# RMSNorm at the layer boundary and at the end: one root per token column, spread by a matmul; last tiles split

## Chip, cores, metric

One NeuronCore of a Trainium2 chip. The metric is the device time of one execution in microseconds; the runs of the kernel before gave 1078.87 us as median of three (1077.52 to 1078.99).

## What is computed

A backbone of two layers over 512 latent and 256 context tokens of width 1024. Layer 0 is a Fourier mixer, layer 1 a bidirectional retention with four heads. Each branch is normed, modulated, gated and projected back; what comes out is the normed latent stream.

```python
def rmsnorm(x, g):
    return x * lax.rsqrt(jnp.mean(x * x, axis=-1, keepdims=True) + EPS) * g
for i in range(2):
    hl = rmsnorm(x, norm_g[i]) * (1.0 + sc_l) + sh_l      # 512 latent tokens
    hc = rmsnorm(ctx, norm_g[i]) * (1.0 + sc_c) + sh_c    # 256 context tokens
    if i == 0:
        ol, oc = fourier_mixer(hl, ...), fourier_mixer(hc, ...)   # both end in @ w_out (2048 x 1024)
    else:
        ol, oc = retention_mixer(hl, hc, ...)
    x = x + gt_l * ol
    if i == 0:
        ctx = ctx + gt_c * oc
return rmsnorm(x, final_g)
```

## The kernel before

Activations lie with features on the 128 partitions and tokens along the free axis: eight feature tiles (KT = 8) of 512 latent columns (LAT) and 256 context columns, together 768 (TOK). Each product is made in three single-precision matmuls of a high and a low part of both operands (`mm3`, L1373 to L1375). The weights come as a stream of slots of 128x1024; each is loaded by the sync engine, converted to its high part by ScalarE (`hi`, L578) and its low part made by VectorE (`lo`, L903), in halves of 512 columns, into a ring of two slots. TensorE waits for the halves (`split`) and frees them (`slot_done`). Every engine executes its own list in order; the order was written by hand, and semaphores join the lists.

Layer boundary. `out_tile` makes one 128-feature tile of the out0 projection: for each of 16 k tiles, three matmuls of the 512 latent columns, then three of the 256 context columns with the same weights, into two accumulator banks. For each finished tile m VectorE adds the gated result to x (`x1_tile`, L1121), ScalarE squares it (L719) and makes a scaled copy tmp_t (L720), and VectorE adds the squares to acc_t (`x1_squares`, L1129). After the last tile TensorE multiplies acc_t by a matrix of ones (L1604 latent, L1606 context). Every partition then holds the sums of all tokens, 128x512 and 128x256. ScalarE roots them to rstd_t (`root`, L743), VectorE inverts them (reciprocal L1153 for the latents, L1175 for the context, before `h1_norm(3)`).

Then h = tmp_t * rstd + shift is made tile by tile: the multiplication for latents on VectorE (`h1_norm`, L1160), for latent tiles 2 and 5 and for all eight context tiles on GpSimd (L520, L525), the high part on ScalarE (`h1_hi`, L751), the low part on VectorE (`h1_low`, L1166). First all eight latent steps, then all eight context steps. Behind them, on ScalarE and on VectorE, stands `used(0)` of head 0, which converts head slot 2. TensorE's `head(0, first=True)` multiplies slots 0 and 1 with the latents (`lat_pair(0, 0, 1)`, one k as soon as `hlo_done` says so), then slots 2 and 3 (`lat_pair(2, 7, 6)`), and then slots 4 and 5 with latents and context.

End. The out1 projection has eight tiles of 512 columns. After each: `x2_tile` (L1335), square on ScalarE (L865), `x2_squares` (L1342). After the last: sums by the matrix of ones (L1700), root (L884), reciprocal (L1362), and the products with the rstd and final_g: five tiles on VectorE (L1365), three on GpSimd (L566). The sync engine stores each tile of 128x512.

Near the start, GpSimd makes an identity of 128x128 (L460, L462) inside the `gate` buffer, after VectorE has finished part of the layer-0 input. VectorE scales it to diagonals (L1053), and TensorE multiplies these by the ones (L1519), which spreads a value per token over all partitions.

## Time and profile before

| | |
|---|---|
| median of 3 runs | 1078.87 us |
| span of the profiled execution | 1077.0 us |
| TensorE matmul | 1007.6 us busy (94%) |
| VectorE | 519.9 us (48%) |
| ScalarE | 408.2 us (38%) |
| GpSimd | 197.6 us (18%) |
| mean granted TensorE clock | 0.976 of full |
| DMA | 98.14 MB, 91 GB/s on average |

The page's second part cuts the span into 40 slices of 27 us and gives the busy share of each engine in tenths; a dip of TensorE's row is where something other than matmuls may set the time. A timeline row gives the start, the length and, in brackets, the idle time of that engine before the row with the instruction that ended it. Rows of one kind that follow each other are merged (x2, x11), so their length is that of all. Matmuls overlap, so the distance between two starts is the cost of one, not its length.

### The profile page before, as it was taken

To read this page: it belongs to the slowest core of one execution; us is meant where nothing else is said; L and a number is where in the kernel's file an instruction comes from. 1 tells how busy PE (TensorE), PEld (TensorE's weight loads), DVE (VectorE), ACT (ScalarE), POOL (GpSimd) and SP (SyncE) were. 2 spreads that over 40 slices of the span, in tenths; PEclk is the share of its full clock that TensorE was granted. 3 is DMA by queue.
4 is the path that set the end of the run, shared out by engine and by line. 5 is a ranking of instruction groups with operands and counts; after the bars stand their busy time and mean duration, and the time that the engine had idled before them with its cause. 6 is when DMAs were issued, how large, how long until landed. Compare 5 with 4: busy or idle time off the path is not lost.

```text
span 1077.0 us, 14382 instructions
## 1 busy us (share of the span) xinstructions
PE 1007.6 (94%) x5186; PEld 840.2 (78%) x5186; DVE 519.9 (48%) x812; ACT 408.2 (38%) x750; POOL 197.6 (18%) x240
## 2 busy tenths in 40 slices
PE   2798999999999999999599999999999999998993
PEld 2678999777777788888488888888888878886882
DVE  5658444533555363332845426542644264446434
ACT  7347433433544343222433323332333233352321
POOL 3006323122443230000400013001300130010001
PEclk9898999999999999999899999999999999998997
DMA  7642112153534352122021102210221021101222
GB/s 275 250 162 74 60 62 97 42 173 119 165 129 148 125 201 93 60 78 78 20 91 66 61 19 79 76 59 19 78 78 58 19 78 58 58 20 59 98 79 78
DMA packets 27417, 98.14 MB, mean 91 GB/s; under 512 B 3664, under 2 KB 3696, under 8 KB 26992
## 3 DMA queue, kind: packets, MB, share of 16 engines
q1 hardware_dynamic: 25632, 90.77, 25.0%
q0 software_dynamic: 1744, 6.84, 1.7%
q8 instruction: 24, 0.39, 0.1%
q14 instruction: 17, 0.14, 0.0%
HBM read 95.48 MB, written 2.10 MB: 91 GB/s over the span
## 4 chain that ended last, share of the span: by engine, by line
PE 83%; DVE 9%; POOL 3%; ACT 2%; DMA 1%; issue 1%; SPq 0%; DVEq 0%; POOLq 0%; ACTq 0%
PE banks L1373 27%; PE banks L1374 27%; PE banks L1375 26%; DVE ring L903 2%; PE banks L1447 2%; ACT ring L578 1%; DVE hreg L1166 1%; POOL gate L541 1%; POOL gate L462 1%; DMA raw<-stream 1%; DVE xreg L1225 1%; DMA gate<-x_rows 1%; DVE gate L1160 1%; DVE hreg L978 1%; DVE xreg L1365 0%
## 5 line engine op out<-in xcount | busy, mean ns | idle before, releaser
L903 DVE TENSOR_TENSOR ring<-raw,ring 128x512 fp32r<-128x512 f32 x320 | 220.2, 718 | 366.7 <-ACT ring L578 365.0
L578 ACT ACTIVATE ring<-raw 128x512 fp32r<-128x512 f32 x320 | 190.0, 626 | 399.4 <-PE banks L1375 382.6
L1373 PE MATMUL banks<-hreg,ring 128*128 128x512 f32 (+1 forms) x800 | 291.2, 364 | 19.8 <-DVE hreg L1166 9.1
L1374 PE MATMUL banks<-hreg,ring 128*128 128x512 f32 (+1 forms) x800 | 287.6, 360 | 0.0
L1375 PE MATMUL banks<-hreg,ring 128*128 128x512 f32 (+1 forms) x800 | 285.7, 357 | 0.0
L1373 PEld LDWEIGHTS banks<-hreg,ring 128*128 128x128 f32 x800 | 151.9, 190 | 56.1 <-DVE ring L903 18.1
L1375 PEld LDWEIGHTS banks<-hreg,ring 128*128 128x128 f32 x800 | 151.5, 189 | 23.3
L1374 PEld LDWEIGHTS banks<-hreg,ring 128*128 128x128 f32 x800 | 151.9, 190 | 22.4 <-issue 1.0
L1373 PE MATMUL banks<-wreg,ring 128*128 128x258 f32 (+2 forms) x288 | 93.1, 323 | 10.3 <-DVE ring L903 9.2
L1374 PE MATMUL banks<-wreg,ring 128*128 128x258 f32 (+2 forms) x288 | 92.7, 322 | 0.0
L1375 PE MATMUL banks<-wreg,ring 128*128 128x258 f32 (+2 forms) x288 | 92.2, 320 | 0.0
L501 POOL TENSOR_TENSOR gate<-xreg,gate 128x257 f32<-128x257 f32 (+1 forms) x64 | 50.2, 814 | 135.3 <-ACT gate L688 126.0
L1373 PE MATMUL banks<-ring,hreg 128*128 128x512 f32 x192 | 74.7, 389 | 0.0
L1374 PE MATMUL banks<-ring,hreg 128*128 128x512 f32 x192 | 74.7, 389 | 0.0
L1375 PE MATMUL banks<-ring,hreg 128*128 128x512 f32 x192 | 74.7, 389 | 0.0
L1373 PEld LDWEIGHTS banks<-wreg,ring 128*128 128x128 f32 x288 | 55.1, 191 | 15.3 <-issue 11.1
L534 POOL TENSOR_TENSOR gate<-gate 128x512 f32<-128x512 f32 x12 | 16.7, 1395 | 250.7 <-ACT gate L768 249.9
L1375 PEld LDWEIGHTS banks<-wreg,ring 128*128 128x128 f32 x288 | 55.0, 191 | 4.2
L1374 PEld LDWEIGHTS banks<-wreg,ring 128*128 128x128 f32 x288 | 55.2, 192 | 3.8
L1373 PE MATMUL banks<-wreg 128*128 128x512 f32 x144 | 56.0, 389 | 0.0
L1374 PE MATMUL banks<-wreg 128*128 128x512 f32 x144 | 56.0, 389 | 0.0
L1375 PE MATMUL banks<-wreg 128*128 128x512 f32 x144 | 56.0, 389 | 0.0
(174 smaller groups left out, 1290.3 us busy)
## 6 DMA issues: line engine op xcount, KB each, us to landing
raw<-stream SPq DMA_DIRECT2D x160, 512.0 KB, 3.3
gate<-x_rows SPq DMA_DIRECT2D x6, 512.0 KB, 9.3
gate<-x_lat POOLq DMA_DIRECT2D x1, 2048.0 KB, 14.4
xreg<-x_lat POOLq DMA_DIRECT2D x1, 2048.0 KB, 7.8
xreg<-tables_in SPq DMA_DIRECT2D x1, 1284.0 KB, 10.2
out<-xreg SPq DMA_DIRECT2D x5, 256.0 KB, 2.6
gate<-x_ctx POOLq DMA_DIRECT2D x1, 1024.0 KB, 18.1
xreg<-x_ctx POOLq DMA_DIRECT2D x1, 1024.0 KB, 11.0
```

The lines of the kernel that those rows point to most:

```text
L462: pool.affine_select(out=ident, in_=ident, compare_op=ALU.not_equal, fill=1.0, base=0, pattern=[[-1, P]], channel_multiplier=1).then_inc(i ...
L501: pool.tensor_tensor(g, y, g, ALU.mult).then_inc(gated, 1)
L534: pool.tensor_tensor(head_rstd, head_rstd, p_f[:, i % 2, :], ALU.add).then_inc(oacc, 1)
L541: pool.tensor_tensor(g, g, p_f[:, i % 2, :], ALU.mult).then_inc(ogated, 1)
L578: act.activation(ring[:, n % 2, 0, c], raw[:, buf, c], ACT.Copy).then_inc(hi_done, 1)
L903: dve.tensor_tensor(ring[:, n % 2, 1, c], raw[:, buf, c], f32(ring[:, n % 2, 0, c]), ALU.subtract).then_inc(split_done, 1)
L978: dve.scalar_tensor_tensor(out=xs[1][:, t, :], in0=x_tok[:, t, :], scalar=tok_rstd[:, t:t + 1], in1=f32(xs[0][:, t, :]), op0=ALU.mult, op1 ...
L1160: dve.tensor_tensor(tmp_t[:, k, 0:LAT], tmp_t[:, k, 0:LAT], rstd_t[:, 0:LAT], ALU.mult).then_inc(t_vec, 1)
L1373: pe.matmul(out, left[0], right[0], start=start, stop=False)
L1374: pe.matmul(out, left[0], right[1], start=False, stop=False)
L1375: return pe.matmul(out, left[1], right[0], start=False, stop=stop)
L1447: last = pe.matmul(bank(7, parts=4), cond[:, k, :], ring[:, par, part, 512 * half:512 * half + 512], start=k == 0 and part == 0, stop=k == ...
```

## The change

The sums of squares are taken per token as a column: a matmul whose stationary operand is a 128-token block of acc_t and whose moving operand is one column of ones gives 128 tokens on 128 partitions (`token_sums`). ScalarE roots a 128 x n block with one column per 128 tokens (n is 4 for the latents, 2 for the context or a half of the latents) and VectorE inverts it; VectorE multiplies an identity by each column (`token_rstd`, result `spread`, 128 x 128n), and TensorE multiplies the matrix of ones by these diagonals (`token_rows`). For the latents this is written to two banks: one is read by VectorE directly, the other is copied to rstd_t by ScalarE (`rstd_copy`) for GpSimd.

The last out0 tile does all 16 k of the latent columns first and then all 16 k of the context columns (`out_last`); the latent sums are taken inside the context part, after k = 9. The context sums are taken inside the first pair of head 0, after k = 4; their root stands on ScalarE after `h1_hi(4)`, their inversion on VectorE before `h1_norm(7)`, `token_rows(1)` on TensorE after the whole first pair, and the copy for GpSimd on ScalarE after the last latent `h1_hi`. The conversion of head slots 0 and 1 moves behind the last out0 tile's context part on both engines.

The last out1 tile is made in two halves of 256 tokens, each with its own sums, root, spread and output products. Stores are one transfer for several tiles of a half: tiles 3 to 5 and 6 to 7 from the sync engine, tiles 0 to 2 from ScalarE's queue. The identity gets a buffer of its own and is made without the wait for the layer-0 input.

The diff, cut (declarations, the `parts` argument of `x1_tile` and `x1_squares` and unchanged lines are left out):

```diff
+        ident = sb("ident", [P, P])
...
+        spread = gate[:, 6144:6144 + TOK].rearrange("p (t n) -> p t n", t=TT)
+        tok_rms = small[:, 0:TT]
...
-            for m in range(KT):
-
-                if m < POOL_TILES:
-                    sp.wait_ge(out_pool, m + 1)
-                    src = tmp_t[:, m, 0:LAT]
-                else:
-                    sp.wait_ge(out_vec, m - POOL_TILES + 1)
-                    src = x3[:, m, :]
-                sp.dma_start(out[m], src).then_inc(s_out, 16)
-            sp.wait_ge(s_out, 16 * KT)
+            for h in range(2):
+                c = slice(LAT // 2 * h, LAT // 2 * (h + 1))
+                for a, b in ((POOL_TILES, 6), (6, KT)):
+                    sp.wait_ge(out_vec, (KT - POOL_TILES) * h + b - POOL_TILES)
+                    sp.dma_start(out[a:b].rearrange("m p t -> p m t")[:, :, c],
+                                 x3[:, a:b, c]).then_inc(s_out, 16)
+            sp.wait_ge(s_out, 16 * 6)
...
-            pool.wait_ge(hf_lo, KT + 1)
-            pool.memset(ident, 0.0).then_inc(ident_set, 1)
+            pool.memset(ident[:, :], 0.0).then_inc(ident_set, 1)
...
-            pool.affine_select(out=ident, in_=ident, compare_op=ALU.not_equal, fill=1.0, base=0,
+            pool.affine_select(out=ident[:, :], in_=ident[:, :], compare_op=ALU.not_equal, fill=1.0, base=0,
...
             gate_head(HEADS - 1, (0, 2))
-            pool.wait_ge(rstd_done, 3)
-            for m in range(POOL_TILES):
-                pool.wait_ge(gained, m + 1)
-                pool.tensor_tensor(tmp_t[:, m, 0:LAT], tmp_t[:, m, 0:LAT], rstd_t[:, 0:LAT],
-                                   ALU.mult).then_inc(out_pool, 1)
+            for h in range(2):
+                c = slice(LAT // 2 * h, LAT // 2 * (h + 1))
+                pool.wait_ge(rstd_done, 3 + h)
+                for m in range(POOL_TILES):
+                    pool.wait_ge(gained, m + 1)
+                    pool.tensor_tensor(tmp_t[:, m, c], tmp_t[:, m, c], rstd_t[:, c],
+                                       ALU.mult).then_inc(out_pool, 1)
         @block.scalar
...
             hi("out0", 5, SLOT_OUT0 + 5)
-            def x1_tile(m, q):
-
-                for v, (a, b, x) in enumerate(((0, LAT, x3), (LAT, TOK, xc3))):
+            def root(n, first, tiles):
+                act.wait_ge(sum_sq_done, n + 1)
+                act.activation(tok_rms[:, first:first + tiles], bank(4, tiles, first), ACT.Sqrt,
+                               scale=1.0 / D, bias=eps[:, :]).then_inc(root_done, 1)
+
+            def rstd_copy(n, a, b, src):
+                act.wait_ge(rows_spread, n + 2)
+                act.activation(rstd_t[:, a:b], src, ACT.Copy).then_inc(rstd_done, 1)
+
+            def x1_tile(m, q, parts=(0, 1)):
+
+                for v in parts:
+                    a, b, x = ((0, LAT, x3), (LAT, TOK, xc3))[v]
                     act.wait_ge(x1_done, 2 * m + (v + 1 + 4))
...
             act.activation(dk[:, 1, 0:1], eps[:, :], ACT.Sqrt).then_inc(warm, 1)
+            x1_tile(7, 1, (0,))
+            root(0, 0, 4)
+            x1_tile(7, 1, (1,))
             hi("head", 0, SLOT_HEAD)
             hi("head", 1, SLOT_HEAD + 1)
-            x1_tile(7, 1)
-
-            def root(n, a, b):
-                act.wait_ge(sum_sq_done, n + 1)
-                act.activation(rstd_t[:, a:b], banks[:, a:b], ACT.Sqrt, scale=1.0 / D,
-                               bias=eps[:, :]).then_inc(root_done, 1)
             def h1_hi(k, v, a, b):
...
                                bias=mod1[:, 8 + k, v:v + 1]).then_inc(hhi_done, 1)
-            root(0, 0, LAT)
-            root(1, LAT, TOK)
+            rstd_copy(0, 0, LAT, bank(7))
             for k in range(KT):
                 h1_hi(k, 0, 0, LAT)
+                if k == 4:
+                    root(1, 4, 2)
+            rstd_copy(1, LAT, TOK, bank(3, CTX))
             for k in range(KT):
...
-            x2_sq(7, 1)
-            act.wait_ge(sum_sq_done, 3)
-            act.activation(rstd_t[:, 0:LAT], bank(0), ACT.Sqrt, scale=1.0 / D,
-                           bias=eps[:, :]).then_inc(root_done, 1)
+            act.wait_ge(acc_done, 7 + (2 * KT + 4))
+            for h in range(2):
+                c = slice(LAT // 2 * h, LAT // 2 * (h + 1))
+                act.wait_ge(x2_half, h + 1)
+                act.activation(sq_t[:, 1, c], x3[:, KT - 1, c], ACT.Square).then_inc(sq_half, 1)
+                act.wait_ge(sum_sq_done, 3 + h)
+                act.activation(tok_rms[:, 2 * h:2 * h + 2], bank(0, 2, 2 * h), ACT.Sqrt, scale=1.0 / D,
+                               bias=eps[:, :]).then_inc(root_done, 1)
+                act.wait_ge(rows_spread, 5 + 2 * h)
+                act.activation(rstd_t[:, c], bank(3 + 2 * h, LAT // 2), ACT.Copy).then_inc(rstd_done, 1)
+            for h in range(2):
+                c = slice(LAT // 2 * h, LAT // 2 * (h + 1))
+                act.wait_ge(out_pool, POOL_TILES * (h + 1))
+                act.dma_start(out[0:POOL_TILES].rearrange("m p t -> p m t")[:, :, c],
+                              tmp_t[:, 0:POOL_TILES, c]).then_inc(s_out, 16)
...
+            dve.wait_ge(hf_lo, 12)
...
-                dve.tensor_scalar(diag[:, t, :], ident, tok_rstd[:, t:t + 1], None,
+                dve.tensor_scalar(diag[:, t, :], ident[:, :], tok_rstd[:, t:t + 1], None,
...
-            for q in range(2):
-                if q == 0:
-                    lo("out0", 14, SLOT_OUT0 + 14)
-                    lo("out0", 15, SLOT_OUT0 + 15)
-                else:
-                    lo("head", 0, SLOT_HEAD)
-                x1_tile(6 + q, (bank(3 + 2 * q), bank(4 + 2 * q, CTX)), SLOT_OUT0 + 13 + 2 * q)
-                x1_squares(6 + q, q)
+            lo("out0", 14, SLOT_OUT0 + 14)
+            lo("out0", 15, SLOT_OUT0 + 15)
+            x1_tile(6, (bank(3), bank(4, CTX)), SLOT_OUT0 + 13)
+            x1_squares(6, 0)
+
+            def token_rstd(n, first, tiles):
+
+                dve.wait_ge(root_done, n + 1)
+                r = tok_rms[:, first:first + tiles]
+                link(dve.reciprocal(r, r))
+                dve.tensor_tensor(spread[:, first:first + tiles, :],
+                                  ident[:, :].unsqueeze(1).to_broadcast([P, tiles, P]),
+                                  r.unsqueeze(2).to_broadcast([P, tiles, P]),
+                                  ALU.mult).then_inc(spread_done, 1)
+
+            last_banks = bank(5), bank(6, CTX)
+            dve.wait_ge(last_lat, 1)
+            x1_tile(7, last_banks, None, (0,))
+            x1_squares(7, 1, (0,))
+            dve.wait_ge(glo, FT)
+            dve.wait_ge(ident_set, 2)
+            token_rstd(0, 0, 4)
+            x1_tile(7, last_banks, SLOT_OUT0 + 15, (1,))
+            x1_squares(7, 1, (1,))
+            lo("head", 0, SLOT_HEAD)
...
-            dve.wait_ge(root_done, 1)
-            dve.reciprocal(rstd_t[:, 0:LAT], rstd_t[:, 0:LAT]).then_inc(rstd_done, 1)
-            dve.wait_ge(rstd_done, 1)
+            dve.wait_ge(rows_spread, 1)
...
-                    dve.tensor_tensor(tmp_t[:, k, 0:LAT], tmp_t[:, k, 0:LAT], rstd_t[:, 0:LAT],
+                    dve.tensor_tensor(tmp_t[:, k, 0:LAT], tmp_t[:, k, 0:LAT], bank(2),
...
             for k in range(KT):
-                if k == 1:
-                    dve.wait_ge(root_done, 2)
-                    dve.reciprocal(rstd_t[:, LAT:TOK], rstd_t[:, LAT:TOK]).then_inc(rstd_done, 1)
+                if k == 5:
+                    token_rstd(1, 4, 2)
                 h1_norm(k + 2)
...
-            for q in range(2):
-                if q == 0:
-                    lo("out1", 14, SLOT_OUT1 + 14)
-                    lo("out1", 15, SLOT_OUT1 + 15)
-                x2_tile(6 + q, 7 - q, SLOT_OUT1 + 13 + 2 * q)
-                x2_squares(6 + q, q)
-            dve.wait_ge(root_done, 3)
-            dve.reciprocal(rstd_t[:, 0:LAT], rstd_t[:, 0:LAT]).then_inc(rstd_done, 1)
-            dve.wait_ge(rstd_done, 3)
-            for m in range(POOL_TILES, KT):
-                dve.scalar_tensor_tensor(out=x3[:, m, :], in0=x3[:, m, :], scalar=g_final[:, m:m + 1],
-                                         in1=rstd_t[:, 0:LAT], op0=ALU.mult,
-                                         op1=ALU.mult).then_inc(out_vec, 1)
+            lo("out1", 14, SLOT_OUT1 + 14)
+            lo("out1", 15, SLOT_OUT1 + 15)
+            x2_tile(6, 7, SLOT_OUT1 + 13)
+            x2_squares(6, 0)
+
+            def last_out(h):
+
+                c = slice(LAT // 2 * h, LAT // 2 * (h + 1))
+                dve.wait_ge(rows_spread, 4 + 2 * h)
+                for m in range(POOL_TILES, KT):
+                    dve.scalar_tensor_tensor(out=x3[:, m, c], in0=x3[:, m, c],
+                                             scalar=g_final[:, m:m + 1], in1=bank(1 + h, LAT // 2),
+                                             op0=ALU.mult, op1=ALU.mult).then_inc(out_vec, 1)
+
+            for h in range(2):
+                c = slice(LAT // 2 * h, LAT // 2 * (h + 1))
+                if h == 0:
+                    dve.wait_ge(last_half, 1)
+                else:
+                    dve.wait_ge(slot_done, 2 * SLOTS + DONE0)
+                dve.scalar_tensor_tensor(out=x3[:, KT - 1, c], in0=bank((6, 4)[h], LAT // 2),
+                                         scalar=mod1[:, 24 + KT - 1, 0:1], in1=x3[:, KT - 1, c],
+                                         op0=ALU.mult, op1=ALU.add).then_inc(x2_half, 1)
+                dve.wait_ge(sq_half, h + 1)
+                dve.wait_ge(acc_done, KT - 1 + (2 * KT + 5))
+                dve.tensor_tensor(acc_t[:, c], acc_t[:, c], sq_t[:, 1, c], ALU.add).then_inc(acc_half, 1)
+                if h == 0:
+                    dve.wait_ge(glo, 2 * FT)
+                token_rstd(2 + h, 2 * h, 2)
+                last_out(h)
...
-            with pe.Fori(2, 4) as jj:
+            with pe.Fori(2, 3) as jj:
...
-            pe.wait_ge(acc_done, 2 * KT + 3)
-            pe.matmul(bank(0), ones[:, :], acc_t[:, 0:LAT], start=True, stop=True).then_inc(sum_sq_done, 1)
-            pe.wait_ge(acc_done, 2 * KT + 4)
-            pe.matmul(bank(1, CTX), ones[:, :], acc_t[:, LAT:TOK], start=True,
-                      stop=True).then_inc(sum_sq_done, 1)
-
-
+            pe.wait_ge(x1_done, 14)
+            out_tile(SLOT_OUT0 + 12, both_chunks(bank(3), bank(4, CTX)), g0)
+            pe.wait_ge(x1_done, 16)
+
+            def out_last(t, chunks, g, arrived, between):
+
+                for n, (a, b, o) in enumerate(chunks):
+                    for kk in range(FT):
+                        if n == 0 and kk % 4 == 0:
+                            split(t + kk // 8, kk // 4 % 2)
+                        last = mm3(o, part_of(kk // 8, P * (kk % 8)), (g(kk, 0)[:, a:b], g(kk, 1)[:, a:b]),
+                                   kk == 0, kk == FT - 1)
+                        if n == 1 and kk % 4 == 3:
+                            last.then_inc(slot_done, 1)
+                        if n == 1:
+                            between(kk)
+                    if n == 0:
+                        last.then_inc(arrived, 1)
+
+            def token_sums(first, tiles, out):
+
+                for t in range(first, first + tiles):
+                    last = pe.matmul(out[:, t:t + 1], acc_t[:, P * t:P * t + P], ones[:, 0:1],
+                                     start=True, stop=True)
+                last.then_inc(sum_sq_done, 1)
+
+            def token_rows(n, first, tiles, outs):
+
+                pe.wait_ge(spread_done, n + 1)
+                for out in outs:
+                    for t in range(tiles):
+                        last = pe.matmul(out[:, P * t:P * t + P], ones[:, :], spread[:, first + t, :],
+                                         start=True, stop=True)
+                    last.then_inc(rows_spread, 1)
+
+            def lat_sums(kk):
+                if kk == 9:
+                    pe.wait_ge(acc_done, 2 * KT + 3)
+                    pe.wait_ge(x1_done, 18)
+                    token_sums(0, 4, bank(4))
+
+            out_last(SLOT_OUT0 + 14, both_chunks(bank(5), bank(6, CTX)), g0, last_lat, lat_sums)
+            token_rows(0, 0, 4, (bank(2), bank(7)))
...
+            def ctx_sums():
+                pe.wait_ge(acc_done, 2 * KT + 4)
+                token_sums(4, 2, bank(4))
+
...
                 if first:
-                    pe.wait_ge(root_done, 2)
-                    lat_pair(0, 0, 1, KT)
+                    lat_pair(0, 0, 1, KT, between=ctx_sums)
+                    token_rows(1, 4, 2, (bank(3),))
+                    pe.wait_ge(rstd_done, 1)
                 else:
...
-            with pe.Fori(2, 4) as jj:
+            with pe.Fori(2, 3) as jj:
...
-            pe.wait_ge(acc_done, 3 * KT + 5)
-            pe.matmul(bank(0), ones[:, :], acc_t[:, 0:LAT], start=True, stop=True).then_inc(sum_sq_done, 1)
+            pe.wait_ge(x1_done, 2 * 3 + (2 * KT + 3))
+            out_tile(SLOT_OUT1 + 12, ((0, LAT, bank(7)),), g1)
+            pe.wait_ge(x1_done, 2 * 3 + (1 + 2 * KT + 3))
+
+            def half_sums(kk):
+                if kk == 8:
+                    pe.wait_ge(acc_half, 1)
+                    token_sums(0, 2, bank(0))
+                if kk == 14:
+                    token_rows(2, 0, 2, (bank(1), bank(3)))
+
+            out_last(SLOT_OUT1 + 14, ((0, LAT // 2, bank(6, LAT // 2)),
+                                      (LAT // 2, LAT, bank(4, LAT // 2))), g1, last_half, half_sums)
+            pe.wait_ge(acc_half, 2)
+            token_sums(2, 2, bank(0))
+            token_rows(3, 2, 2, (bank(2), bank(5)))
```

## Rows read from the trace of the kernel before

**Rows 1.** The page, part 4: the chain that ended last, its shares by engine
```profile
PE 83%; DVE 9%; POOL 3%; ACT 2%; DMA 1%; issue 1%; SPq 0%; DVEq 0%; POOLq 0%; ACTq 0%
```

**Rows 2.** Timeline, VectorE, layer boundary: start us, us, engine, line, operation, idle before, releaser
```profile
514.07 1.14 DVE L1121 SCALAR_TENSOR_TENSOR xreg<-banks,mod,xreg 128x512 f32<-128x512 f32 x2 [7.04 <-PE banks L1375]
...
518.15 3.35 DVE L1153 RECIPROCAL gate<-gate 128x512 f32<-128x512 f32 x1
521.53 2.36 DVE L1160 TENSOR_TENSOR gate<-gate 128x512 f32<-128x512 f32 x2
...
535.69 5.72 DVE L1166 SCALAR_TENSOR_TENSOR hreg<-gate,mod,hreg 128x512 fp32r<-128x512 f32 x11
541.33 2.48 DVE L903 TENSOR_TENSOR ring<-raw,ring 128x512 fp32r<-128x512 f32 x4
```

**Rows 3.** Timeline, TensorE, layer boundary
```profile
525.72 0.76 PE L1373 MATMUL banks<-hreg,ring 128*128 128x512 f32 x1 [7.90 <-DVE hreg L1166]
...
530.41 0.63 PE L1373 MATMUL banks<-hreg,ring 128*128 128x512 f32 x1
530.84 0.63 PE L1374 MATMUL banks<-hreg,ring 128*128 128x512 f32 x1
...
532.74 0.39 PE L1375 MATMUL banks<-hreg,ring 128*128 128x512 f32 x1
532.97 0.40 PE L1373 MATMUL banks<-hreg,ring 128*128 128x512 f32 x1
...
542.07 0.50 PE L1373 MATMUL banks<-hreg,ring 128*128 128x512 f32 x1 [0.72 <-DVE ring L903]
```

**Rows 4.** Timeline, GpSimd, layer boundary: the eight context norms
```profile
527.31 9.05 POOL L525 TENSOR_TENSOR gate<-gate 128x256 f32<-128x256 f32 x8 [2.29 <-DVE gate L1175]
```

**Rows 5.** Windows: stretch, length, busy us of each engine, PEclk, DMA share, GB/s
```profile
521.00:522.00 1.00, 0.00 (x0) 0.00 (x0) 0.96 (x2) 0.00 (x0) 0.41 (x1) 0.59 0.01 4
```

**Rows 6.** Timeline, all engines, the end of the kernel
```profile
1059.23 0.75 DVE L1335 SCALAR_TENSOR_TENSOR xreg<-banks,mod,xreg 128x512 f32<-128x512 f32 x1 [7.48 <-PE banks L1375]
...
1066.70 6.51 DVE L1365 SCALAR_TENSOR_TENSOR xreg<-xreg,small,gate 128x512 f32<-128x512 f32 x5
```

**Rows 7.** Timeline, VectorE, early in the kernel
```profile
97.07 1.28 DVE L1053 TENSOR_SCALAR gate<-gate,dist 128x128 f32<-128x128 f32 x6 [0.19 <-POOL gate L462]
```

**Rows 8.** Timeline, TensorE, early: 258-column matmuls and the ones x diagonal passes
```profile
99.14 0.28 PE L1374 MATMUL banks<-wreg,ring 128*128 128x258 f32 x1
99.26 0.28 PE L1375 MATMUL banks<-wreg,ring 128*128 128x258 f32 x1
99.76 0.36 PE L1373 MATMUL banks<-wreg,ring 128*128 128x258 f32 x1 [0.22 <-DVE wreg L909]
...
102.71 1.50 PE L1519 MATMUL banks<-gate,ones 128*128 128x128 f32 x12
103.97 0.42 PE L1373 MATMUL banks<-hreg,wreg 128*128 128x386 f32 x1
```

**Rows 9.** Groups by form: line, engine, operation, shapes, count, busy us, mean ns, idle
```profile
L1121 DVE SCALAR_TENSOR_TENSOR xreg<-banks,mod,xreg 128x256 f32 x4 | 1.9, 474 | 0.0
...
L961 DVE RECIPROCAL dist<-dist 128x1 f32<-128x1 f32 x6 | 0.9, 158 | 3.4 <-ACT dist L601 3.4
...
L578 ACT ACTIVATE ring<-raw 128x512 fp32r<-128x512 f32 x320 | 190.0, 626 | 399.4 <-PE banks L1375 382.6 <-DMA raw<-stream 11.5 <-PE banks L1447 4.4
...
L751 ACT ACTIVATE hreg<-gate,mod 128x256 fp32r<-128x256 f32 x8 | 3.3, 494 | 0.0
...
L601 ACT ACTIVATE dist<-dist,eps 128x1 f32<-128x1 f32 x6 | 1.8, 294 | 0.2
...
L551 POOL TENSOR_TENSOR xreg<-xreg 128x512 f32<-128x512 f32 x8 | 10.4, 1297 | 0.0
```

**Rows 10.** Timeline, 650 to 665 us: VectorE reads a bank while GpSimd works
```profile
653.53 1.27 DVE L1190 TENSOR_TENSOR gate<-banks,gate 128x512 f32<-128x512 f32 x2
...
653.69 1.29 POOL L549 TENSOR_TENSOR xreg<-xreg 128x512 f32<-128x512 f32 x1 [10.08 <-DVE xreg L1225]
```

17 lines of the change are left out of this document (11 added, 6 removed).

## Prediction

> **What bounds the kernel now.** The chain of work that ended last belongs to TensorE for 83% of the span [rows 1], and TensorE is busy nearly everywhere at the full clock. A change of norms can therefore only act where TensorE stands still. I read the page's slices for the two dips (the layer boundary at 514 to 542 us and the end from 1059 us), then the timelines of each engine there, then the groups by form for durations.
>
> At the boundary VectorE starts on the last out0 tile at 514.07, the moment TensorE has finished it. It converts its last head-slot part at 518.1, takes 3.35 us for a reciprocal over 128x512, and begins the norms at 521.53 [rows 2]. TensorE starts layer 1 at 525.72, and its second pair of columns of head 0 at 542.07, after 0.72 us of waiting for a ring part (L903) [rows 3]. That part is queued on VectorE behind all sixteen h1_low steps (the last eleven start at 535.69 and the ring follows at 541.33) [rows 2]. So until 542.07 the bound is VectorE's queue, not TensorE. Beside it GpSimd does the eight context norms from 527.31 to 536.36, while the latent half is still going on [rows 4]. That overlap is what matters below.
>
> TensorE's granted clock falls to half within 521 to 522, after about 3.4 us in which it had done nothing (its sums ended 7.90 us before 525.72, at 517.8) [rows 3, 5]. After the restart matmuls stand 0.43 us apart (530.41, 530.84), later 0.23 (532.74, 532.97) [rows 3]. Between 525.72 and 531.3 some 12 matmuls ran at 1.2 GHz instead of 2.4, 0.2 us each: a restart from a cold clock costs 2.4 us.
>
> At the end, the last matmul is over at 1059.2. From there a chain of whole 512-token steps: x2 at 1059.23, square, add, sums, root, a reciprocal as long as the first, and then five output tiles on VectorE from 1066.70 for 6.51 us (1.3 us each while GpSimd works beside it) and then 3.8 us until the span's end at 1077.0 [rows 6].
>
> **Start of the kernel.** The identity moves to a buffer of its own and is made some 50 us earlier. VectorE no longer waits for it at 97.07, 0.19 us [rows 7]; TensorE waited 0.22 us at 99.76 for the weights that VectorE makes next [rows 8]. I take -0.2 (bounds 0 and -0.3). GpSimd stood idle where the instruction goes now.
>
> **Boundary, up to the first matmul of layer 1.** The latent chunk of the last tile goes first, the context chunk after it, so the same matmuls end where they did. Between them TensorE makes four column sums: 4 x 2 passes of at most one short pass. Twelve passes of 128 columns took 1.26 us from 102.71 to 103.97, 0.105 each [rows 8], so 0.9 us (from 0.3, as one column streams in less, to 2.8, if none overlaps the next: one alone takes 1.50 less eleven starts of 0.105, 0.35). x1 of the latents, squares, sums, the small root, the small reciprocal (158 ns for one column [rows 9]) and the spread over the identity are hidden under the 5.6 us of the context chunk. TensorE ends the tile at about 515.0.
>
> What is late next is not the norm but VectorE's queue: x1 of the context waits for the chunk's end (0.47), ScalarE squares and scales it (two steps of under 0.49), and only then converts four ring halves, 0.6 each, which VectorE follows (0.69 for the last) [rows 9]. 515.0 + 0.5 + 0.9 + 2.4 + 0.7 = 519.4 against 521.53: of the 3.35 us reciprocal only 2.1 us come back.
>
> The first two norms read a bank now. VectorE's steps with one operand in a bank stayed at 0.63 us apiece while GpSimd worked beside them (653.53, two in 1.27; GpSimd's 1.29 unchanged) [rows 10], whereas the same norms from SBUF took 1.18 each [rows 2]. So the first h1_low ends about 2.8 us after the norms begin, instead of 4.0, and TensorE starts at 522.2 (was 525.72). It has been idle 5.4 us, longer than the 3.4 us above, and starts at half clock, as before.
>
> **Boundary, step 5.** At the half clock TensorE does k = 0, 1 until 527.4, then k = 2 to 4 at 1.38 each until 531.5, then the context sums (0.45). VectorE is ahead of it now, as it has no long reciprocal and cheaper norms. But its next step, token_rstd(1), sits in front of norm 7 and h1_low 5, and waits for the root of those context sums. Behind TensorE's sums at 532.0 come the root (0.29, as for one column), reciprocal (0.16) and spread (0.45), norm 7 (0.62), h1_low 5 (0.7) and hops [rows 9, 10]: TensorE idles 2.4 us and does k = 5 to 7 from 534.4 to 538.5.
>
> **Boundary, the context half: the term that decides.** Before, the context's rstd was ready at 527.3 [rows 4] and GpSimd multiplied under the latent half. Now token_rows(1) stands on TensorE behind the whole first pair of head 0. Only after it come ScalarE's copy to rstd_t, which stands behind all latent h1_hi, GpSimd's eight norms, h1_hi and h1_low of the context; and behind these, on ScalarE and on VectorE, the conversion of head slot 2, without which TensorE can't start the second pair. Nothing covers this chain:
> - token_rows(1), 4 passes of 0.11: 539.0. ScalarE's copy with hops 0.5: 539.5.
> - GpSimd, eight 128x256 products. They took 1.13 each beside a busy VectorE [rows 4]. Alone, 128x512 takes 1.30 [rows 9], so half of it at least 0.65; with some fixed part I take 0.74. VectorE would have one 0.47 us step per tile here, so I take 0.74 + 7 x 1.0 = 7.7: 547.3 (bounds 545.4 and 548.6).
> - h1_hi 0.5, h1_low 0.5, the ring half 0.7, hops: 1.8. TensorE restarts at 549.1, against 542.07: +7.0 us.
> - This idle time is 10 us, so the clock is at half once more: +2.4 us, which before did not occur here.
>
> Together the boundary gives +9.4 us. Later TensorE is unbroken in head 0, so it is all carried on.
>
> For the contention, the row (1.13 beside a VectorE that never paused) bounds the step from above. The Trainium skill, page "SBUF — State Buffer", section "Who interferes with whom", says more: a VectorE instruction with two SBUF inputs and a GpSimd instruction that reads SBUF exclude one another wholly. By that each step would take 0.74 + 0.43, the context chain would be 1.2 us longer, and the total 1086.6. The same section has a VectorE instruction with one SBUF input free of GpSimd, and the 653.53 row agrees.
>
> **End.** The last tile is done in halves of 256 tokens. Same columns in all; 258 columns stood 0.12 apart (99.14, 99.26) [rows 8], so 96 matmuls need 11.4 instead of 10.9 us. The sums of half 0 (0.45) and its rows (0.9, before the last k) come on top: TensorE ends at about 1061.1 (was 1059.2). Half 0: rows at about 1060.3, then VectorE's five products, 0.47 each with a bank operand [rows 9]: 1062.6. The chain of half 1 stands behind these on VectorE, 1.5 us later than its matmuls allow. Then x2 0.47, square 0.45, add 0.45, sums 0.7, root 0.3, reciprocal and spread 0.65, rows 0.7 (slow clock), hops 0.3: 1066.6. VectorE's products end at 1069.0; the second copy for GpSimd is behind the rows' second set, 1067.9, and its three products of 0.74 end at 1070.1. With the 3.8 us that followed the last product before, and 0.4 for larger transfers of 1 KB pieces (no row shows one: bounds -0.3 and +1.5), the span ends 2.7 us earlier (bounds 1.2 and 3.7).
>
> **The sum.** +9.4 - 2.7 - 0.2 = +6.5 us on the execution of 1077.0: 1083.5. The median of the runs is 1.9 us above that profile, so 1085.4 us. Unknown terms: GpSimd's rate -1.9/+1.3; the second cold restart -2.4; the wait at k = 5, if the clock falls in it too, +2.4; the end -1/+1.5. This gives 1082 to 1089.
>
> **Rivals.**
> - The context chain is hidden (the forecast's main step is wrong): if slot 2 were ready when the first pair ends, the pair would follow at 539.0, 3.1 us earlier than before, and the time would be 1078.9 - 3.1 - 0.2 - 2.7 = 1072.9. For it: the code gives the chain the same covers as before by name. Against: the in-order queues. It decides once the chain from 538.5 takes under 3.5 us, where GpSimd alone needs 5.2. Chance 0.08.
> - The chain is there but cheap: products at 0.7, warm restart, the full gain at the end: 1085.4 - 1.9 - 2.4 - 1 = 1080.1, no difference to be told. Chance 0.12.
> - The clock falls a third time, at k = 5: 1087.8. Speaking for it, at 521 to 522 it fell after 3.4 us idle; against, this wait is 2.4. Part of the forecast's range, 0.15.
> - The change doesn't do what it says: the reciprocals don't shorten, as the small steps' fixed costs add up. Each is 0.16 to 0.45, far below 3.35; inside the range too.
>
> **How the numbers follow.** Forecast (slower, 1082 to 1089) 0.80, within it the centre; the no-difference case 0.12; the faster one 0.08. A measurement here tells about 0.2%, 2.2 us. For 8 in 10 the range reaches from 1080.0 to 1089.5.
>
> **What would show it.** Right: TensorE's first hreg matmul near 522, an idle time of 2 to 3 us before k = 5, a wait of 8 to 11 us before the second pair with GpSimd's eight products inside it, a granted clock at half after it, a last product near 1070. Wrong: context products that start before TensorE has ended the first pair, or a second pair that starts by 543.

## The result and the profile after

The changed kernel took 1088.05 us (median of four runs, 1084.60 to 1088.15) beside 1078.93 us for the kernel before on the same chip: a ratio of 1.0078, 95% interval 1.0058 to 1.0097. Measured again on another chip it took 1084.81 us (six runs, 1083.66 to 1088.11) beside 1079.53: 1.0047, 1.0029 to 1.0065. It is slower, by 5 to 9 us. The profiled execution took 1084.60 us, with a span of 1082.8 us, and TensorE's mean granted clock was 0.973 (0.976 before).

The chain that ended last, page part 4, shares by engine. Beside [rows 1], "issue" went from 1% to 3% and VectorE from 9% to 7%:

```profile
PE 84%; DVE 7%; POOL 3%; issue 3%; ACT 2%; DMA 1%; SPq 0%; POOLq 0%; DVEq 0%; ACTq 0%
```

The timeline of TensorE at the boundary after the change (it answers to [rows 3]; in brackets the idle time and what ended it):

```profile
510.68 0.95 PE L1683 MATMUL banks<-ones,gate 128*128 128x1 f32 x8
...
521.37 0.76 PE L1431 MATMUL banks<-hreg,ring 128*128 128x512 f32 x1 [5.70 <-DVE hreg L1208]
...
530.79 0.50 PE L1683 MATMUL banks<-ones,gate 128*128 128x1 f32 x4
533.55 0.80 PE L1431 MATMUL banks<-hreg,ring 128*128 128x512 f32 x1 [2.27 <-DVE hreg L1208]
534.15 0.63 PE L1432 MATMUL banks<-hreg,ring 128*128 128x512 f32 x1
534.58 0.63 PE L1433 MATMUL banks<-hreg,ring 128*128 128x512 f32 x1
...
539.32 0.61 PE L1692 MATMUL banks<-gate,ones 128*128 128x128 f32 x4
549.15 0.77 PE L1431 MATMUL banks<-hreg,ring 128*128 128x512 f32 x1 [9.22 <-DVE ring L926]
```

There are three waits here: 5.70 us before the layer's first matmul (7.90 before [rows 3]), 2.27 us at k = 5 behind the context's column sums (L1683), and 9.22 us before the second pair. The last one was 0.72 us before [rows 3].

The other engines in the same stretch, each from its own timeline (VectorE answers to [rows 2], GpSimd to [rows 4]):

```profile
512.06 0.18 DVE L1179 RECIPROCAL small<-small 128x4 f32<-128x4 f32 x1 [2.63 <-ACT small L718]
...
518.22 1.28 DVE L1202 TENSOR_TENSOR gate<-gate,banks 128x512 f32<-128x512 f32 x2
...
531.62 0.17 DVE L1179 RECIPROCAL small<-small 128x2 f32<-128x2 f32 x1 [5.95 <-ACT small L718]
...
546.83 0.57 DVE L1208 SCALAR_TENSOR_TENSOR hreg<-gate,mod,hreg 128x256 fp32r<-128x256 f32 x1 [0.29 <-ACT hreg L761]
547.69 0.48 DVE L1208 SCALAR_TENSOR_TENSOR hreg<-gate,mod,hreg 128x256 fp32r<-128x256 f32 x1 [0.29 <-ACT hreg L761]
548.31 2.50 DVE L926 TENSOR_TENSOR ring<-raw,ring 128x512 fp32r<-128x512 f32 x4
```

```profile
540.42 6.69 POOL L526 TENSOR_TENSOR gate<-gate 128x256 f32<-128x256 f32 x8 [19.75 <-ACT gate L723]
```

```profile
539.96 0.38 ACT L723 ACTIVATE gate<-banks 128x256 f32<-128x256 f32 x1 [6.37 <-PE banks L1692]
541.18 0.51 ACT L761 ACTIVATE hreg<-gate,mod 128x256 fp32r<-128x256 f32 x1 [0.83 <-POOL gate L526]
541.87 0.51 ACT L761 ACTIVATE hreg<-gate,mod 128x256 fp32r<-128x256 f32 x1 [0.17 <-POOL gate L526]
542.82 0.51 ACT L761 ACTIVATE hreg<-gate,mod 128x256 fp32r<-128x256 f32 x1 [0.45 <-POOL gate L526]
543.69 0.51 ACT L761 ACTIVATE hreg<-gate,mod 128x256 fp32r<-128x256 f32 x1 [0.36 <-POOL gate L526]
```

The 3.35 us reciprocal is gone (0.18), and VectorE's norms start at 518.22 instead of 521.53 (the whole boundary lies 0.94 us earlier in this execution, see the table below). But the context's chain now begins only when TensorE has ended the pair: rows 539.32, copy 539.96, GpSimd 540.42 to 547.11, ring part 548.31, TensorE 549.15. GpSimd had been idle for 19.75 us; before, it did the same eight products at 527.31 [rows 4].

The granted clock by stretch (columns as in [rows 5]: length, busy us of the five engines, then PEclk):

```profile
531.50:533.50 2.00, 0.00 (x0) 0.00 (x0) 1.85 (x5) 1.93 (x4) 0.00 (x0) 1.00 0.00 0
534.00:536.00 2.00, 2.00 (x6) 1.52 (x6) 0.82 (x2) 0.00 (x0) 0.00 (x0) 0.50 0.03 8
...
538.00:542.00 4.00, 1.93 (x11) 1.49 (x9) 0.28 (x1) 1.03 (x3) 1.57 (x3) 1.00 0.00 0
...
544.00:549.00 5.00, 0.00 (x0) 0.00 (x0) 3.47 (x7) 3.57 (x8) 3.12 (x4) 0.50 0.00 0
549.00:552.00 3.00, 2.85 (x7) 2.33 (x8) 3.00 (x7) 0.74 (x2) 0.00 (x0) 0.50 0.41 115
```

Each new wait is followed by a stretch at half clock (1.2 GHz). In the short one the granted clock still stands at 1.00 until 533.50, as the wait ends; the matmuls behind it run at 0.50.

The end, from the timelines of VectorE, TensorE and GpSimd (they answer to [rows 6]), and from the page's part 6 the two stores that ScalarE issues (size and median time from issue to landing):

```profile
1058.70 0.75 DVE L1376 SCALAR_TENSOR_TENSOR xreg<-banks,mod,xreg 128x512 f32<-128x512 f32 x1
...
1069.47 2.05 DVE L1406 SCALAR_TENSOR_TENSOR xreg<-xreg,small,banks 128x256 f32<-128x256 f32 x5 [1.71 <-PE banks L1692]
1071.43 0.48 DVE L1416 SCALAR_TENSOR_TENSOR xreg<-banks,mod,xreg 128x256 f32<-128x256 f32 x1
...
1076.15 2.05 DVE L1406 SCALAR_TENSOR_TENSOR xreg<-xreg,small,banks 128x256 f32<-128x256 f32 x5 [1.31 <-PE banks L1692]
```

```profile
1068.82 1.05 PE L1692 MATMUL banks<-gate,ones 128*128 128x128 f32 x8
1072.87 1.01 PE L1683 MATMUL banks<-ones,gate 128*128 128x1 f32 x4 [2.64 <-DVE gate L1421]
1074.89 2.07 PE L1692 MATMUL banks<-gate,ones 128*128 128x128 f32 x8 [1.01 <-DVE gate L1180]
```

```profile
1077.46 2.09 POOL L569 TENSOR_TENSOR gate<-gate 128x256 f32<-128x256 f32 x3 [5.00 <-ACT gate L903]
```

```profile
out<-gate ACTq DMA_DIRECT2D x2, 384.0 KB, 2.7
```

**Where the time went.** Two moments cut the span the same way in every kernel here: TensorE's first 258-column matmul after the modulation, and the start of VectorE's x2 of out1 tile 6 (L1335 before, L1376 after). The three stretches, and the time from the latent column sums (L1683 x8) to that x2 for the kernels that have them, read from each kernel's timelines:

| kernel | to the first 258-column matmul | from there to x2 of tile 6 | rest of the span | latent sums to x2 of tile 6 |
|---|---|---|---|---|
| before | 96.50 | 953.13 | 27.37 | |
| changed | 95.56 | 963.14 | 24.10 | 548.02 |
| changed, again | 97.01 | 962.81 | 24.08 | 547.29 |
| only the boundary | 95.61 | 963.02 | 27.37 | 547.73 |
| only the end | 99.13 | 952.97 | 23.90 | |
| context sums early | 96.40 | 959.83 | 23.87 | 544.98 |
| wait filled | 95.33 | 960.33 | 24.04 | 545.15 |
| ring first | 96.72 | 958.83 | 23.75 | 543.32 |
| whole context chain early | 96.58 | 946.26 | 24.06 | 531.18 |
| same, filled | 97.00 | 946.40 | 22.80 | 530.79 |
| same, end woven | 94.62 | 946.19 | 23.19 | 531.09 |
| reordered | 94.34 | 948.67 | 23.19 | 531.61 |
| reordered, filled | 94.55 | 945.68 | 23.17 | 530.33 |

So between the two profiled executions the change is -0.94, +10.01 and -3.27 us, together the 5.8 us of the spans. The first column varies from 94.34 to 99.13 among the twelve rows below "before", whose code is the same in that stretch, so it measures no part of the change. It goes with the granted clock of one early stretch: from 50 to 60 us that was 1.00 in the six executions with 94.34 to 95.61 us in this column, the changed kernel's first among them, 0.83 to 0.86 in the six with 96.40 to 97.01, and 0.70 in "only the end".

### The profile page after: what moved, and what is told of

Its sections match the earlier page's. It is cut to its first block, busy times and chain, and to the rows that moved or that the text cites. A ratio compares the mean times of both kernels' runs of the same rounds, so it can differ in the third digit from the quotient of the medians.

```text
span 1082.8 us, 14568 instructions
## 1 busy us (share of the span) xinstructions
PE 1016.4 (94%) x5284; PEld 853.1 (79%) x5284; DVE 508.4 (47%) x824; ACT 410.0 (38%) x756; POOL 186.8 (17%) x243
## 4 chain that ended last, share of the span: by engine, by line
PE 84%; DVE 7%; POOL 3%; issue 3%; ACT 2%; DMA 1%; SPq 0%; POOLq 0%; DVEq 0%; ACTq 0%
PE banks L1431 28%; PE banks L1432 27%; PE banks L1433 27%; DVE ring L926 3%; PE banks L1505 2%; ACT ring L581 1%; DMA raw<-stream 1%; POOL gate L542 1%; DVE hreg L1051 1%; DVE xreg L1266 1%; POOL gate L526 1%; DVE hreg L1001 1%; DVE gate L1231 0%; POOL gate L535 0%; POOL xreg L552 0%
## 5 line engine op out<-in xcount | busy, mean ns | idle before, releaser
L1431 PE MATMUL banks<-hreg,ring 128*128 128x512 f32 (+1 forms) x812 | 295.0, 363 | 27.2 <-DVE ring L926 16.8
L1432 PE MATMUL banks<-hreg,ring 128*128 128x512 f32 (+1 forms) x812 | 291.1, 359 | 0.0
L1433 PE MATMUL banks<-hreg,ring 128*128 128x512 f32 (+1 forms) x812 | 289.1, 356 | 0.0
L1431 PEld LDWEIGHTS banks<-hreg,ring 128*128 128x128 f32 x812 | 155.2, 191 | 61.4 <-issue 19.2
L1433 PEld LDWEIGHTS banks<-hreg,ring 128*128 128x128 f32 x812 | 154.8, 191 | 23.1
L1432 PEld LDWEIGHTS banks<-hreg,ring 128*128 128x128 f32 x812 | 155.3, 191 | 22.5 <-issue 1.0
L1431 PE MATMUL banks<-wreg,ring 128*128 128x258 f32 (+2 forms) x292 | 94.3, 323 | 9.2 <-DVE ring L926 9.0
L1432 PE MATMUL banks<-wreg,ring 128*128 128x258 f32 (+2 forms) x292 | 93.8, 321 | 0.0
L1433 PE MATMUL banks<-wreg,ring 128*128 128x258 f32 (+2 forms) x292 | 93.3, 319 | 0.0
L1431 PEld LDWEIGHTS banks<-wreg,ring 128*128 128x128 f32 x292 | 56.3, 193 | 14.2 <-issue 10.2
L535 POOL TENSOR_TENSOR gate<-gate 128x512 f32<-128x512 f32 x12 | 16.8, 1396 | 250.7 <-ACT gate L780 250.0
L1433 PEld LDWEIGHTS banks<-wreg,ring 128*128 128x128 f32 x292 | 56.3, 193 | 3.9
L1432 PEld LDWEIGHTS banks<-wreg,ring 128*128 128x128 f32 x292 | 56.4, 193 | 3.7
```

Source lines behind the costliest of these rows:

```text
L535: pool.tensor_tensor(head_rstd, head_rstd, p_f[:, i % 2, :], ALU.add).then_inc(oacc, 1)
L1431: pe.matmul(out, left[0], right[0], start=start, stop=False)
L1432: pe.matmul(out, left[0], right[1], start=False, stop=False)
L1433: return pe.matmul(out, left[1], right[0], start=False, stop=stop)
```

## The experiments

**Only the end**: the kernel before with the identity's own buffer and the last out1 tile in halves.

```diff
+        ident = sb("ident", [P, P])
...
-            dve.wait_ge(root_done, 3)
-            dve.reciprocal(rstd_t[:, 0:LAT], rstd_t[:, 0:LAT]).then_inc(rstd_done, 1)
...
+            for h in range(2):
...
+                token_rstd(2 + h, 2 * h, 2)
+                last_out(h)
```

> The end of the changed kernel and its own identity buffer, with the layer boundary of the kernel before. If the sum of the prediction holds, the end and the start give -2.7 and -0.2 us: 1076.0 us on 1078.9 (the traces of before and after, cut at the add of out1 tile 6, say -3.3: 1075.4). Rival: the end gives nothing by itself, as the last transfers and the second half's chain take it back: 1078.7.

1074.67 us (six runs, 1074.19 to 1077.84), ratio 0.9951 (0.9938 to 0.9964). The end alone is a gain: 27.37 to 23.90 us in the table. (The profiled execution was the longest of the six, 1077.84 us, by its first stretch.)

**Only the boundary**: the changed kernel with the end of the kernel before.

```diff
-            for h in range(2):
...
-                token_rstd(2 + h, 2 * h, 2)
-                last_out(h)
...
+            dve.wait_ge(root_done, 3)
+            dve.reciprocal(rstd_t[:, 0:LAT], rstd_t[:, 0:LAT]).then_inc(rstd_done, 1)
```

> The boundary of the changed kernel, with the end of the kernel before. Forecast of the sum: +9.4 - 0.2, so 1088.1 us; the second pair of head 0 starts 7 us later than in before, behind a wait of 9 us with GpSimd's eight context products in it. Rival: most of the loss of the changed kernel lies elsewhere (more instructions outside loops, the end): under 1083.

1087.76 us (six runs, 1086.46 to 1089.21), ratio 1.0071 (1.0057 to 1.0086). The middle stretch is 963.02 against 953.13, the end unchanged to the hundredth. The two halves of the change are thus separate, and the loss is all in the boundary. The two ratios add up to +0.22%, with some 0.2% of uncertainty, which fits the +0.47% of the second measurement and not the +0.78% of the first; the stretches of the profiled executions do add up (963.14 and 24.10 beside 963.02 and 23.90).

**The whole context chain early**: the changed kernel, with the context's column sums, root, reciprocal, spread and rows ahead of the first pair, and ScalarE's copy behind its first h1_hi. Nothing is added, only moved.

```diff
# TensorE
-                    lat_pair(0, 0, 1, KT, between=ctx_sums)
+                    ctx_sums()
                     token_rows(1, 4, 2, (bank(3),))
+                    lat_pair(0, 0, 1, KT)
# VectorE
+            token_rstd(1, 4, 2)
             dve.wait_ge(rows_spread, 1)
...
-                if k == 5:
-                    token_rstd(1, 4, 2)
# ScalarE
+            root(1, 4, 2)
             rstd_copy(0, 0, LAT, bank(7))
...
-                if k == 4:
-                    root(1, 4, 2)
-            rstd_copy(1, LAT, TOK, bank(3, CTX))
+                if k == 0:
+                    rstd_copy(1, LAT, TOK, bank(3, CTX))
```

> The changed kernel, with the context's column sums, root, inversion, spread and rows all made before the first pair of head 0, in the time in which TensorE waits for h1 anyway, and ScalarE's copy of the context rows after h1_hi(0). If the serial context chain behind the first pair is the cause, both waits (2.3 us at k = 5, 9.2 us before the second pair) and one or two cold restarts go: the rival's sum, 1072.9 us, plus 0.6 for VectorE's extra steps before the first norm: 1073.5. If the contention or the banks as operands are the cause, the loss stays: over 1080.

1067.29 us (six runs, 1066.06 to 1071.26), ratio 0.9887 (0.9869 to 0.9905): 12 us below the kernel before, 17 to 21 below the changed one. Its timelines, TensorE, VectorE and GpSimd:

```profile
520.74 0.96 PE L1691 MATMUL banks<-gate,ones 128*128 128x128 f32 x4 [3.75 <-DVE gate L1180]
522.97 0.77 PE L1430 MATMUL banks<-hreg,ring 128*128 128x512 f32 x1 [1.26 <-DVE hreg L1209]
```

```profile
519.39 1.29 DVE L1180 TENSOR_TENSOR gate<-ident,small 128x256 f32<-128x256 f32 x1
```

```profile
522.39 7.68 POOL L526 TENSOR_TENSOR gate<-gate 128x256 f32<-128x256 f32 x8 [0.57 <-ACT gate L723]
```

GpSimd's eight products again run under the latent half, and TensorE does not wait in either place. The first matmul comes 11.31 us after the latent sums instead of 10.69, so the move costs 0.6 us ahead of the layer. The result is 6 us better than I had expected, and the fault was in the expectation: it started from the forecast's 538.5 us for the end of the first pair, a time that contains the wait at k = 5. That wait and its half clock went too. From the rows: 539.32 to 549.15 is 9.83 us, its restart 2.0 (ten matmuls 0.43 instead of 0.23 us apart), 530.79 to 533.55 is 2.76, its restart 1.4 (seven such), less 0.6: 15.4 of the 16.8 us in the table's last column. Where the other 1.4 us went stays open.

**Context sums early, the rest late**: the same with the rows and the copy left behind the first pair, so that only the wait at k = 5 is taken away.

```diff
# against the changed kernel
-                    lat_pair(0, 0, 1, KT, between=ctx_sums)
+                    ctx_sums()
+                    lat_pair(0, 0, 1, KT)
                     token_rows(1, 4, 2, (bank(3),))
```

> The changed kernel, with the context's column sums, root, inversion and spread made before the first pair of head 0, but its rows, ScalarE's copy and all behind them still after the pair. It parts the two waits. The wait at k = 5 (2.27 us) and the half clock after it (534 to 537, 1.5 us) go, less 0.6 us of steps before the first norm: 3 us less than the changed kernel. The wait of 9.2 us and its cold restart stay. If instead the contention of GpSimd with VectorE were the main loss, nothing changes.

1082.05 us (twelve runs, 1079.58 to 1084.61), ratio 1.0024 (1.0011 to 1.0036), 2.8 us below the changed kernel measured beside it. The second wait is untouched:

```profile
545.88 0.77 PE L1429 MATMUL banks<-hreg,ring 128*128 128x512 f32 x1 [9.22 <-DVE ring L925]
```

With the 0.6 us paid ahead of the layer taken off, the wait at k = 5 and its half clock are worth 3 us (963.0 to 959.8 in the table; by the last column 2.3 to 3.0), the late rows and copy the other 13.6 (959.83 to 946.26).

**The wait filled**: nine 512-column matmuls, whose result nothing uses, on TensorE between the rows and the second pair. All else as changed.

```diff
                     token_rows(1, 4, 2, (bank(3),))
+                    for _ in range(9):
+                        pe.matmul(bank(5), ones[:, :], acc_t[:, 0:LAT], start=True, stop=True)
                     pe.wait_ge(rstd_done, 1)
```

> The changed kernel, with nine matmuls of 512 columns on ones and acc_t into a free bank, their result unused, put into TensorE's 9.2 us wait before the second pair. They shorten no chain. If the clock's fall is worth 2.4 us there, the second pair runs at full clock and the time falls by 2.4 us (-0.2%) against the changed kernel; if the cost lies in the wait alone, it doesn't move.

1081.71 us (twelve runs, 1079.26 to 1085.07), ratio 1.0017 (1.0004 to 1.0029). TensorE's timeline and the window of the wait:

```profile
539.53 7.89 PE L1725 MATMUL banks<-gate,ones 128*128 128x512 f32 x18
548.93 0.47 PE L1431 MATMUL banks<-hreg,ring 128*128 128x512 f32 x1 [1.51 <-DVE ring L926]
```

```profile
544.00:549.00 5.00, 3.49 (x9) 1.26 (x8) 3.68 (x7) 3.59 (x8) 2.90 (x4) 1.00 0.00 0
549.00:556.00 7.00, 7.00 (x31) 5.79 (x32) 4.94 (x8) 1.53 (x4) 2.53 (x2) 1.00 0.47 150
```

The second pair comes when it came before (548.93, 549.15), but at the full clock. Latent sums to x2 of tile 6 is 545.15 against 548.02 and 547.29: the second cold restart costs 2.1 to 2.9 us, as the forecast had it (2.4). The chain itself sets the start of the pair.

**The changed kernel again**, on the same chip as "context sums early" and the next two:

> The changed kernel itself once more, on the chip of the three that follow, so that they can be held against it. Its first runs gave 1084.6 and three times 1088.1, the mean clock 0.973 and 0.970: expect 1087 us, and longer runs to be those with the lower mean clock (0.003 of 1083 us is 6.5 us more at half speed, worth 3.2 us). If the length doesn't follow the clock, the spread has another cause.

1084.81 us (1083.66 to 1088.11), 1.0047; I had expected 1087. Both new waits are there again to the hundredth (9.22, 2.27). Its runs lie at 1084 to 1086 with a clock of 0.972 or 0.973, and one at 1088.11 with 0.970, as three of the first four did. So the longer run is the one with the lower clock, as expected. The kernel before does likewise, 1077 to 1081.5. No trace was taken of a longer run of either kernel. The one trace of a long run, "only the end" (1077.84 us on a median of 1074.67), has the excess in the first 100 us, where TensorE's clock fell early on (the table's first column); whether that holds for the other long runs stays open.

**The early chain, filled**: four unused matmuls in the 3.75 us wait and one behind it.

> The version with the early context rows (1067.3 us), with four unused matmuls of 512 columns in TensorE's 3.75 us wait before the context rows, and one behind them. If the half clock after that wait costs time (11 matmuls 0.43 us apart instead of 0.23), the clock stays up and the time falls by up to 2.2 us: 1065.1. Rival: TensorE at full clock then only waits for h1_low, one step each 1.3 to 2 us, and nothing is gained: 1067.3.

1067.25 us (four runs, 1066.67 to 1068.04), ratio 0.9881, against 1067.29 without. The clock stayed at 1.00 through the boundary, yet next to nothing was gained up to the end (530.79 beside 531.18 in the table's last column), because TensorE, now sooner, met VectorE's queue:

```profile
536.78 0.47 PE L1430 MATMUL banks<-hreg,ring 128*128 128x512 f32 x1 [1.61 <-DVE ring L926]
```

It is the bound of the kernel before once more (0.72 us at 542.07, [rows 3]): a ring part behind all sixteen h1_low. The time didn't fall to the 1065.1 that a full clock alone would give; the rival that I had named held.

**The end woven**: the early chain, and in the last tile x2 and add of half 1 put between the output products of half 0; the second rows go first to the bank that ScalarE copies.

```diff
+            last_x2(0)
+            last_add(0)
...
+            last_out(0, POOL_TILES, 5)
+            last_x2(1)
+            last_out(0, 5, 6)
+            last_add(1)
+            last_out(0, 6, KT)
```

> The version with the early context rows, with the end reordered: VectorE's x2, add of the second half go in between the five products of the first half, and the second half's rows go to ScalarE's bank first. If the second half's chain is bound by its place behind the first half's products on VectorE, as the prediction has it, x2 of half 1 comes 1.1 us earlier and the end some 1 to 1.3 us: 1066.2. If its bound is the last matmul or the stores, it stays at 1067.3.

1066.05 us (four runs, 1065.58 to 1066.60), ratio 0.9872 (0.9854 to 0.9891). VectorE's timeline:

```profile
1045.29 0.48 DVE L1415 SCALAR_TENSOR_TENSOR xreg<-banks,mod,xreg 128x256 f32<-128x256 f32 x1 [2.35 <-PE banks L1443]
...
1052.37 0.48 DVE L1415 SCALAR_TENSOR_TENSOR xreg<-banks,mod,xreg 128x256 f32<-128x256 f32 x1
```

x2 of half 1 starts 7.08 us after that of half 0 instead of 8.24 (1063.19 to 1071.43 in the changed kernel), and the rest of the span is 23.19 against 24.06 us: 0.9 of the 1.5 us that the forecast had put on this queue. The difference to the early chain alone lies within the intervals of the medians; the traces show it, the times do not. And the clock matters as much at this place. The filled early chain has the unwoven end and needs only 22.80 us for it, less than the woven one. Its last rows ran at the full clock, 1.20 us where those of the other kernels, the woven ones included, took 2.07 or 2.08:

```profile
1059.19 1.20 PE L1691 MATMUL banks<-gate,ones 128*128 128x128 f32 x8 [1.01 <-DVE gate L1180]
```

That is the one of the eight traces with the unwoven end in which the clock did not fall there. No run says why.

**The ring first**: the changed kernel, with the conversion of head slots 2 and 3 moved ahead of the context's copy, h1_hi and h1_low on ScalarE and VectorE. This asks whether the queue behind which slot 2 stands is the cause, rather than the lateness of the context's rstd.

```diff
# ScalarE
+            hi("head", 2, SLOT_HEAD + 2)
+            hi("head", 3, SLOT_HEAD + 3)
             rstd_copy(1, LAT, TOK, bank(3, CTX))
# VectorE
+            lo("head", 2, SLOT_HEAD + 2)
+            lo("head", 3, SLOT_HEAD + 3)
             for k in range(KT):
                 h1_low(k, 1, LAT, TOK)
```

> The changed kernel, with nothing moved but the conversions of head slots 2 and 3: on ScalarE and on VectorE they now stand before the context's copy, h1_hi and h1_low, not behind them. The context chain is as long as it was and still follows the first pair. If the loss is the place of the ring conversions in the two queues behind that chain, the wait of 9.2 us before the second pair and its cold restart (2.4 us) go, and the chain hides under the second pair's 11 us, a last 0 to 1 us of it perhaps before the third pair: 1084.8 - 9.2 - 2.4 + 0.5 = 1073.7. If TensorE needed the context's parts themselves, or the chain were lengthened by the same amount, the time stays near 1084.

1079.96 us (twelve runs, 1078.92 to 1084.53), ratio 1.0022 (1.0006 to 1.0038): some 4 us won in the trace (543.32 beside 547.29 and 548.02 in the table; 2.7 by the two ratios), not the 11 expected. The wait before the second pair is gone, so the second pair itself needs nothing of the context. But the next one took its place, before the third pair. ScalarE, GpSimd, VectorE and TensorE:

```profile
540.45 0.63 ACT L581 ACTIVATE ring<-raw 128x512 fp32r<-128x512 f32 x1 [2.13 <-PE banks L1441]
540.99 0.37 ACT L723 ACTIVATE gate<-banks 128x256 f32<-128x256 f32 x1
```

```profile
541.43 7.03 POOL L526 TENSOR_TENSOR gate<-gate 128x256 f32<-128x256 f32 x8 [19.21 <-ACT gate L723]
```

```profile
549.44 2.47 DVE L1272 TENSOR_TENSOR xreg<-banks,gate 128x512 f32<-128x512 f32 x4
```

```profile
556.62 0.77 PE L1439 MATMUL banks<-hreg,ring 128*128 128x512 f32 x1 [4.86 <-DVE ring L930]
```

The second half of slot 3 can be converted only when TensorE releases its place at the pair's end (ScalarE 540.45). Behind it stands the context's copy (540.99), which is no later than it was: 28.8 us after the latent sums, 29.3 in the changed kernel. GpSimd, h1_low, the rotation (549.44) and the next ring part follow it in turn, and all of that is longer than the second pair covers. My expectation had looked at the first consumer only. The late rstd is the cause; the order behind it decides which pair of columns pays.

**Reordered, cold and filled**: end_woven's code with the context's root, reciprocal and spread ahead of the conversion of slot 1, and slot 2 converted ahead of the context's h1_low; the second kernel adds the five unused matmuls.

```diff
# VectorE
-            lo("head", 1, SLOT_HEAD + 1)
             token_rstd(1, 4, 2)
+            lo("head", 1, SLOT_HEAD + 1)
...
+            lo("head", 2, SLOT_HEAD + 2)
             for k in range(KT):
                 h1_low(k, 1, LAT, TOK)
```

> The version with early context rows and the reordered end (1066.1 us), with the context's root and spread before the conversion of slot 1, so that the spread runs before GpSimd starts (0.43 us instead of 1.29), and slot 2 converted before the context's h1_low. TensorE starts about 0.7 us earlier and never waits for slot 2; its restart is still cold: 1065.3.

> The same, with five unused matmuls in TensorE's wait before layer 1. With the late start alone (1067.3 without and with them) the full clock only brought a wait of 1.6 us for slot 2. That slot now is early, so the full clock should count here: 2 us less, 1063.5. If h1_low paces TensorE's first pair at either clock, there is no gain: 1065.3.

1067.12 us (0.9891, 0.9873 to 0.9909) and 1065.71 us (0.9884, 0.9865 to 0.9903), where I had expected 1065.3 and 1063.5. The reordering won nothing: TensorE's first matmul comes 11.5 us after the latent sums in both, not 0.7 us sooner than the 11.3 of the early chain. VectorE:

```profile
516.54 1.29 DVE L928 TENSOR_TENSOR ring<-raw,ring 128x512 fp32r<-128x512 f32 x2 [0.49 <-ACT ring L581]
...
517.94 0.42 DVE L1182 TENSOR_TENSOR gate<-ident,small 128x256 f32<-128x256 f32 x1
518.28 2.35 DVE L928 TENSOR_TENSOR ring<-raw,ring 128x512 fp32r<-128x512 f32 x2
```

The spread takes 0.42 us instead of the 1.29 it took beside GpSimd, but the two ring steps behind it now meet GpSimd instead and take 2.35 us, where the two ahead of it took 1.29. The contention was moved, not removed. With the wait filled, the table's last column is the shortest of all (530.33). End woven and this one are some 1.2% faster than the kernel before and are not told apart by their times.

**The identity late**: the kernel before, its identity in a buffer of its own but still made where it was. One run, and one of the kernel before beside it.

```diff
+        ident = sb("ident", [P, P])
...
-            pool.affine_select(out=ident, in_=ident, ...
+            pool.affine_select(out=ident[:, :], in_=ident[:, :], ...
```

> The kernel before, with the identity in a buffer of its own but made at the old place, after VectorE's ninth low part (L1028). GpSimd's affine select took 9.63 us there in before and 0.29 us in the changed kernel, where VectorE was idle at its start. If VectorE's unbroken row of steps with two SBUF operands holds GpSimd off, it takes 9.6 us again; if it was the place of the buffer, 0.3 us.

1079.62 us beside 1078.31, no difference that two single runs can tell. GpSimd's instruction in this kernel, and VectorE's beside it; then the same instruction where the changed kernel has it:

```profile
88.40 9.64 POOL L462 TENSOR_SCALAR_AFFINE_SELECT ident<-ident 128x128 f32<-128x128 f32 x1
```

```profile
84.87 10.61 DVE L1028 SCALAR_TENSOR_TENSOR hreg<-gate,amul,hreg 128x256 fp32r<-128x256 f32 x32
95.39 2.49 DVE L903 TENSOR_TENSOR ring<-raw,ring 128x512 fp32r<-128x512 f32 x4
```

```profile
34.95 0.29 POOL L463 TENSOR_SCALAR_AFFINE_SELECT ident<-ident 128x128 f32<-128x128 f32 x1
```

The long time doesn't come from the buffer. It goes with the moment, or with what the other engines do at it: the instruction ends at 98.04, just after the last of VectorE's unbroken run of 36 steps (97.88), and at 34.95 VectorE was idle.

## Why the prediction was right

It said 1085.4 us, 1080.0 to 1089.5, slower; the two medians are 1088.05 and 1084.81. The profiled span is 1082.8 us, forecast 1083.5. Without the first stretch, which the change doesn't set, the spans differ by +6.7 us, forecast +6.5 with the start's -0.2. The terms behind it hold one by one, but the boundary cost 0.6 more and the end gained 0.6 more than forecast, so that the sum is closer than its terms. Times of before are shifted by the 0.94 us of the first stretch where two kernels are compared.

- **What bounds the kernel** held: only TensorE's waits at the boundary and the end moved the time. In "only the boundary" and "only the end" each stands alone.
- **Start, -0.2.** The identity's instruction shrank from 9.63 to 0.29 us and VectorE's 0.19 us wait went. The 0.94 us by which this stretch was shorter is within what the same code varies by (the clock from 50 to 60 us was 0.83 before and 1.00 after), so the term is not tested.
- **First matmul of layer 1, 522.2 (-3.5).** Measured 521.37, and 525.72 - 0.94 before: -3.4. The forecast's path held in kind: VectorE turned to the norms at 518.22 (forecast 519.4, less the shift 518.5), with the ring parts in its way and not the reciprocal. The norms with a bank operand took 0.64 each beside GpSimd, as [rows 10] said. The page "SBUF — State Buffer" of the Trainium skill, section "Who interferes with whom", has a VectorE instruction with one SBUF input free of GpSimd; these rows agree.
- **Wait at k = 5, 2.4.** It was 2.27, for the reason given (token_rstd(1) behind the context sums). But the clock fell at its end, and seven matmuls ran at the half clock: +1.4 us. The forecast had this as a rival with 0.15 and took the cheaper case, because the wait was shorter than the 3.4 us of [rows 5]. That was the weak step: 2.27 us of waiting behind 0.5 us of one-column sums were enough here, in all five traces that have this wait, some 5 us after TensorE had come back to the full clock. Whether that short stretch mattered was not tried; the 2.23 us wait of the kernel before, at the boundary behind a long stretch of matmuls, left the clock at 1.00. Wait and restart together are 3 us by the run that moved the sums ahead.
- **The context chain, 538.5 to 549.1, is the term that decided**, and the first rival (hidden chain, 1072.9) fell. The chain was where the forecast put it, and shorter: 9.83 us from rows to restart, forecast 10.6. GpSimd took 6.69 us, forecast 7.7: the size of this term was off by 1.0. ScalarE's h1_hi follow GpSimd one by one and show its step: 0.69 us where VectorE's first step hardly overlapped (541.18 to 541.87), 0.95 once (542.82) and 0.87 from then on (543.69). So the step of 0.74 alone was near, the 1.0 beside VectorE too high. VectorE's own step went from 0.48 (547.69, alone) to 0.57. By the exclusion that the same page of the Trainium skill states for a VectorE instruction with two SBUF inputs the step would be 0.69 + 0.48, some 1.2; the rows show 0.87, and the measurement decides: they slow each other by 0.18 and 0.09, and the 1086.6 us worked out from that rule was not the way it went.
- **Second cold restart, +2.4.** Measured 2.0 in the rows and 2.1 to 2.9 by filling the wait.
- The boundary in sum: 549.15 against 542.07 - 0.94 is +8.0 (forecast +7.0: pair ended 1.8 later by the clock fall and small steps, chain 0.8 shorter), and 2.0 for the restart, +10.0 against +9.4.
- **End, -2.7 (1.2 to 3.7).** Measured -3.3. Half 0 went as forecast (x2 of tile 6 to the last product 12.8 us, forecast 13.0). From x2 of half 1 to GpSimd's last product took 8.1, forecast 7.5: the column sums and the first set of rows ran at the half clock and took 1.0 us each (1.01, and half of 2.07 for the two sets), where the forecast had 0.7 each, so VectorE's products began 4.7 us after x2, forecast 4.0. The second set with its copy, and the three products, took what was forecast. The tail behind the last product was 3.25 us, forecast 4.2 (3.8 and 0.4 for the larger stores): the store of 384 KB issued there landed in about 2.7 us. The two errors cancel in part. The last product is at 1079.55 on this page; the "near 1070" of the forecast's signs was counted before the boundary's +9.4 was added (1070.1 + 9.4 - 0.2 = 1079.3).

## What to carry to other kernels

A small step on in-order engines costs what stands behind it, so a sum or a reciprocal that is made cheap can still lose if it is placed where it is easy to issue rather than where its first consumer needs it: here the same instructions, issued some 20 us earlier (the context's rows 9.1 instead of 28.6 us after the latent sums), turned +0.5 to 0.8% into -1.1%. When a chain is moved or a wait taken away, follow it past its first consumer to the next engine's queue (ring first gave back over half of its gain one pair later, the filled early chain nearly all of it). And time a half-clock restart by itself, with filler matmuls, before counting on its return.

## What the runs showed of the hardware

- GpSimd's affine select of 128x128 took 9.63 us beside an unbroken run of 36 VectorE steps with two SBUF operands (9.64 with its own buffer) and 0.29 us at a moment when VectorE was idle: it ended when VectorE's run ended, as if held off by the run as a whole and not by one instruction of it. Its eight 128x256 products took 1.13 us each in the kernel before, 0.96 to 1.12 beside a busy VectorE in the kernels with the early chain (7.68 us for eight, 8.96 in the filled one), 0.84 beside h1_low steps with gaps.
- The granted clock was at 1.2 GHz after a wait of only 2.27 us, in five traces of five; before, it fell some 3.4 us into one [rows 5]. The length of the wait alone does not settle it: after the 2.64 or 2.65 us between the two halves of the end it fell in seven traces of eight.
- Nine matmuls with no use, put into a wait, shortened the kernel by 2.1 to 2.9 us in the trace, as TensorE kept 2.4 GHz.
- A one-column f32 matmul costs nearly as much as a 128-column one: at the full clock eight passes of 128x1 took 0.95 us, eight of 128x128 1.05.
